# The inverse of the triangular 32x32 blocks of a gated DeltaNet chunk: five levels of small matmuls on TensorE, or forward substitution over row pairs on VectorE

## The reference

```
for layer in range(2):
    h = rms_norm(x);  proj = h @ w_in                    # 256 x 1024 times 1024 x 11024
    y_a = latent attention (4 heads)
    y_b = gated DeltaNet (4 heads of 128, chunks of 64)
    y_c = windowed attention, 3 groups of 4 heads (dilations 1, 4, 16)
    x = x + (sum of sigmoid(gate_n) * (y_n * silu(z_n)) @ w_branch[n]) @ w_out
```

```
lower = where(i > j, (k * beta) @ k.T * decay, 0)        # 64 x 64
u, w  = triangular_solve(lower + I, [v * beta, k * beta * exp(gc)])
```

## Time and profile before

| | us |
|---|---|
| median of 3 runs | 794.19 |
| span of the profiled execution | 792.5 |
| what lies around the span (difference to the median) | 1.7 |
| PE busy | 782.7 (99%) |
| DVE busy | 558.1 (70%) |
| ACT busy | 478.0 (60%) |
| POOL busy | 193.1 (24%) |
| mean granted TensorE clock | 0.997 |

### The profile page before, as it was taken

The page is one execution under the profiler, slowest core; times in us unless marked ns, Lnnn a source line. Parts: engine busy times, 40 slices in busy tenths (PEclk is TensorE's granted clock), DMA queues, the critical chain, the costliest instruction groups (busy, mean ns, idle before and its releaser), DMA issues.

```text
span 792.5 us, 15685 instructions
## 1 busy us (share of the span) xinstructions
PE 782.7 (99%) x6298; PEld 674.2 (85%) x6298; DVE 558.1 (70%) x760; ACT 478.0 (60%) x1073; POOL 193.1 (24%) x197
## 2 busy tenths in 40 slices
PE   7999999999999999999999999999999999999998
PEld 6999888878888888888899998888888888888886
DVE  6687878867476477776656886887865754958763
ACT  6869485676486654354457777764856766543551
POOL 1155104206042002321023511221331500116100
PEclk9999999999999999999999999999999999999999
DMA  8666454444463346465565563554455443664551
GB/s 236 197 192 208 157 149 133 152 153 137 133 188 122 114 144 193 123 198 173 156 195 178 160 195 108 170 172 147 130 160 139 132 137 107 183 188 140 187 181 53
DMA packets 73056, 125.16 MB, mean 158 GB/s; under 512 B 9758, under 2 KB 17048, under 8 KB 72984
## 3 DMA queue, kind: packets, MB, share of 16 engines
q1 hardware_dynamic: 72560, 124.10, 51.7%
q10 hardware_dynamic: 423, 0.06, 0.1%
HBM read 122.03 MB, written 1.05 MB: 155 GB/s over the span
## 4 chain that ended last, share of the span: by engine, by line
PE 92%; ACT 3%; DVE 2%; issue 1%; DMA 1%; SPq 0%; ACTq 0%
PE bank L781 23%; PE bank L783 22%; PE bank L782 22%; PE bank L763 3%; PE bank L765 3%; PE bank L764 3%; PE bank L868 2%; PE bank L811 2%; PE bank L921 1%; ACT w_hi L1154 1%; PE bank L882 1%; DMA xs<-in_x 1%; PE bank L916 1%; ACT at L1423 1%; PE bank L898 1%
## 5 line engine op out<-in xcount | busy, mean ns | idle before, releaser
L1488 DVE TENSOR_TENSOR w_lo<-raw,w_hi 128x1024 fp32r<-128x1024 f32 (+4 forms) x240 | 295.9, 1262 | 105.2 <-ACT w_hi L1154 102.8
L1154 ACT ACTIVATE w_hi<-raw 128x1024 fp32r<-128x1024 f32 (+4 forms) x239 | 235.1, 1018 | 89.4 <-PE bank L783 76.7
L781 PE MATMUL bank<-w_hi,hT 128*128 128x512 f32 (+2 forms) x704 | 278.5, 396 | 1.6 <-DVE mixed L1507 1.1
L783 PE MATMUL bank<-w_hi,hT 128*128 128x512 f32 (+2 forms) x704 | 271.5, 386 | 0.0
L782 PE MATMUL bank<-w_lo,hT 128*128 128x512 f32 (+2 forms) x704 | 271.1, 385 | 0.0
L781 PEld LDWEIGHTS bank<-w_hi,hT 128*128 128x128 f32 x704 | 133.5, 190 | 27.5 <-DVE mixed L1507 1.6
L783 PEld LDWEIGHTS bank<-w_hi,hT 128*128 128x128 f32 x704 | 133.1, 189 | 25.7
L782 PEld LDWEIGHTS bank<-w_lo,hT 128*128 128x128 f32 x704 | 133.5, 190 | 22.9
L1942 POOL TENSOR_TENSOR sm<-sm,tab 128x8 f32<-128x8 f32 (+3 forms) x46 | 58.5, 1271 | 184.5 <-ACT dn L1368 78.7
L763 PE MATMUL bank<-hT,w_hi 128*128 128x256 f32 x192 | 54.9, 286 | 0.0
L765 PE MATMUL bank<-hT,w_lo 128*128 128x256 f32 x192 | 54.3, 283 | 0.0
(11 more groups left out here) (233 smaller groups left out, 997.2 us busy)
## 6 DMA issues: line engine op xcount, KB each, us to landing
raw<-in_w_in SPq DMA_DIRECT2D x168, 512.0 KB, 4.5
raw<-in_w_branch SPq DMA_DIRECT2D x24, 512.0 KB, 4.3
raw<-in_w_out SPq DMA_DIRECT2D x16, 512.0 KB, 3.7
raw<-in_w_in SPq DMA_DIRECT2D x8, 384.0 KB, 5.4
raw<-in_w_in SPq DMA_DIRECT2D x8, 320.0 KB, 4.4
raw<-in_mla_w_kv_b SPq DMA_DIRECT2D x8, 256.0 KB, 3.0
raw<-in_mla_w_q_b SPq DMA_DIRECT2D x4, 384.0 KB, 3.3
xs<-in_x SPq DMA_DIRECT2D x2, 512.0 KB, 5.7
```

Source lines behind the costliest of these rows:

```text
L781: mm(o, src[0][:, a, tok], hi[:, k, :], start=starts and p == k == 0, stop=False)
L783: last = mm(o, src[1][:, a, tok], hi[:, k, :], start=False, stop=ends(u, p) and k == k1 - k0 - 1)
L1154: av(view(w_hi, q % SPLIT, k1 - k0, n), view(raw, q % RAW, k1 - k0, n), ACT.Copy).then_inc(hi_done, 1)
L1488: tt(view(w_lo, q % SPLIT, k1 - k0, n), view(raw, q % RAW, k1 - k0, n), view(w_hi, q % SPLIT, k1 - k0, n).bitcast(F32), ALU.subtract).then ...
```

## The change

The five small levels are gone from TensorE and GpSimd. VectorE inverts the 32 diagonal blocks by forward substitution. Three new steps do it.

dn_G, behind unit 25 and ahead of the scores of group 0: the blocks are turned by the vector engine's 32x32 transpose, so that each partition holds the whole matrix of one block (8 blocks of a stack, for each of four groups of 8 result columns), the factors are turned likewise and multiplied in, and two tiles of the result are set to the start values.

dn_S, eight parts behind units 26 to 33, two row pairs each, 16 pairs in all. A pair (the last has only the first of them) is three chained instructions, a multiply-add that finishes the pair's second row, a product of both rows with all rows below, and a reduce that adds them.

dn_T, behind unit 34: a copy that joins the halves, and two transposes that make T and Tt. The step is followed by dn_wide, which waited for the last dn_TX before and now waits for dn_T. dn_X and dn_TX of the level of 32 stay behind units 36 and 37. The table of constants loses the five level masks and the small identity (192 columns) and gains the start values (256).

```diff
-    put(25, ("dn_M", 0))
-
-    for s in range(len(LEVELS)):
-        put(26 + 2 * s, ("dn_X", s))
-        put(27 + 2 * s, *([("dn_M", s + 1)] if s < LAST else [("dn_kd",)] if s == LAST + 1 else []), *([("dn_T1",)] if s == 0 else []), ("dn_TX", s))
-    put(28 + 2 * LAST, ("dn_wide",))
+    put(25, ("dn_G",))
+    for n, pairs in enumerate(solve_parts()):
+        put(SOLVE_FIRST + n, ("dn_S", n))
+    put(SOLVE_FIRST + SOLVE_UNITS, ("dn_T",), ("dn_wide",))
+    put(36, ("dn_X",))
+    put(37, ("dn_kd",), ("dn_TX",))
...
+def solve_parts():
+
+    rows = list(range(0, SUB - 1, 2))
+    cuts = [round(len(rows) * n / SOLVE_UNITS) for n in range(SOLVE_UNITS + 1)]
+    return [rows[a:b] for a, b in zip(cuts, cuts[1:])]
...
             def dn_X(step, layer):
-                s = step[1]
                 b = banks(step)[0]
-                if s <= LAST:
-                    pe.wait_ge(*after("gpsimd", ("dn_M", s), layer))
...
+                pe.wait_ge(*after("vector", ("dn_T",), layer))
                 pe.wait_ge(*free(step, layer))
-                if s > LAST:
-                    last = across(b, lambda o, n, lo, hi: mm(o[hi, :], U_n[lo, n, SUB:CH], d_T[lo, n, :], start=True, stop=True))
-                else:
-                    last = by_rows(b, 0, lambda o, n, r: mm(o, d_Us[r, n, :], const("ident_c")[r, :] if s == 0 else d_T[r, n, :], start=True, stop=True))
-                last.then_inc(bank_full[b], 1)
+                across(b, lambda o, n, lo, hi: mm(o[hi, :], U_n[lo, n, SUB:CH], d_T[lo, n, :], start=True, stop=True)).then_inc(bank_full[b], 1)
...
+            def dn_G(step, layer):
+
+                dve.wait_ge(*after("scalar", ("dn_Uc",), layer))
+                if layer == 0:
+                    dve.wait_ge(start["tab_loaded"], 16)
+                blocks_of = d_Uc.rearrange("p n i -> p i n").unsqueeze(2).broadcast_to([P, SUB, GROUPS_OF, NT * H])
+                nc.vector.transpose(g_L.rearrange("p m i -> p i m"), blocks_of)
+                own_next(nc.vector.transpose(g_b, brk.rearrange("p t h -> p (t h)").unsqueeze(1).broadcast_to([P, GROUPS_OF, NT * H])), layer)
+                stt(g_L, g_L, -1.0, g_b.unsqueeze(1).broadcast_to([P, SUB, SUB]), ALU.mult, ALU.mult)
+                for v in g_T:
+                    last = nc.vector.tensor_copy(v, const("first").rearrange("p (i j) -> p i j", i=SUB))
+                own_next(last, layer)
+
+            def dn_S(step, layer):
+
+                for k in solve_parts()[step[1]]:
+                    j, v = k // GROUPS_OF + 1, k // 2 % 2
+                    old, new = g_T[v], g_T[1 - v]
+                    own_next(stt(old[:, k + 1, 0:j], old[:, k, 0:j], g_L[:, k, k + 1:k + 2], old[:, k + 1, 0:j], ALU.mult, ALU.add), layer)
+                    if k + 2 == SUB:
+                        continue
+                    shape = [P, 2, SUB - k - 2, j]
+                    own_next(tt(planes[v][:, 1:3, k + 2:, 0:j], g_L[:, k:k + 2, k + 2:].unsqueeze(3).broadcast_to(shape),
+                                old[:, k:k + 2, 0:j].unsqueeze(2).broadcast_to(shape), ALU.mult), layer)
+                    own_next(nc.vector.tensor_reduce(new[:, k + 2:, 0:j], planes[v][:, :, k + 2:, 0:j].rearrange("p c i j -> p i j c"), AX.X, ALU.add), layer)
+
+            def dn_T(step, layer):
+
+                own_next(nc.vector.tensor_copy(g_rows[0], g_rows[1]), layer)
+                own_next(nc.vector.transpose(d_T.rearrange("p n (j r) -> p j r n", r=GROUPS_OF), g_T[0].rearrange("p i j -> p j i")), layer)
+                nc.vector.transpose(d_Tt.rearrange("p n i -> p (n i)"), d_T.rearrange("p n j -> p (n j)")).then_inc(part("vector", step), 1)
```

More of the change, by code:

```diff
@@ L328 @@
                   ("inv_n", GROUPS), ("inv_d", 1), ("inv_hd", 1), ("inv_rope", 1), ("eps", 1), ("eps_hd", 1), ("half", 1), ("q_scale", 1),
[L329 to L330 removed]
+                  ("qk_scale", 1), ("power", 1), ("chunk", 2), ("one", 1), ("tri", P), ("same", P), ("not_tri", CH), ("first", SUB * EACH), ("mask_m", 2 * P), ("mask_0", 2 * P), *[(f"mask_{a}", P) for a in APART]):
     TAB[_name] = (_at, _n)
@@ L361, in shape_tables @@
     put("not_tri", np.where(pc <= jc, 0.0, NEG))
[L362 to L369, removed]
+    row, column = np.divmod(np.arange(SUB * EACH)[None, :], EACH)
+    put("first", row == column * GROUPS_OF + i % SUB // EACH)
     for a, prev in (("m", j >= 0 * i), (0, j >= i)):
@@ L1030, in dn_u @@
                 wait_taken(step, layer, ("dn_bT", 2, t))
-                pe.wait_ge(*taken(("dn_TX", LAST + 1), layer))
+                pe.wait_ge(*taken(("dn_TX",), layer))
                 pe.wait_ge(*after("scalar", ("dn_wide",), layer))
@@ L1331, in dn_wide @@
             def dn_wide(step, layer):
-                act.wait_ge(*taken(("dn_TX", LAST), layer))
+                act.wait_ge(*after("vector", ("dn_T",), layer))
                 for c in range(2):
@@ L1340, in dn_kd @@
             def dn_kd(step, layer):
-                act.wait_ge(*full(("dn_X", LAST + 1), layer))
+                act.wait_ge(*full(("dn_X",), layer))
                 act.wait_ge(*taken(("dn_qk",), layer))
@@ L1880, in _ @@
                      "dn_g1": dn_g1, "dn_gc": dn_gc, "dn_row": dn_row, "dn_cv": dn_cv, "dn_silu": dn_silu,
-                     "dn_bT": dn_bT, "dn_bE": dn_bE, "dn_decay": dn_decay, "dn_kkE": dn_kk, "dn_qkE": dn_qk, "dn_X": dn_X, "dn_T1": dn_T1, "dn_TX": dn_TX, "dn_wide": dn_wide, "dn_ws": dn_ws, "dn_ds": dn_ds, "dn_oc": dn_oc, "dn_o": dn_o, "dn_oss": dn_oss,
+                     "dn_bT": dn_bT, "dn_bE": dn_bE, "dn_decay": dn_decay, "dn_kkE": dn_kk, "dn_qkE": dn_qk, "dn_G": dn_G, "dn_S": dn_S, "dn_T": dn_T, "dn_X": dn_X, "dn_TX": dn_TX, "dn_wide": dn_wide, "dn_ws": dn_ws, "dn_ds": dn_ds, "dn_oc": dn_oc, "dn_o": dn_o, "dn_oss": dn_oss,
                      "b_out": b_out, "k_norm": k_norm, "sc": sc, "soft": soft,
@@ L2058, in dn_ss @@
                 last.then_inc(part("gpsimd", step), 1)
-            def dn_M(step, layer):
-                s = step[1]
-                if layer == s == 0:
-                    pool.wait_ge(start["tab_loaded"], 16)
-                pool.wait_ge(*(after("scalar", ("dn_Uc",), layer) if s == 0 else full(("dn_X", s - 1), layer)))
-                tt(d_Us, d_Uc, const(f"levelT{LEVELS[s]}").unsqueeze(1).broadcast_to([P, NT * H, SUB]), ALU.mult).then_inc(part("gpsimd", step), 1)
             def dn_dec(step, layer):
```

72 lines of the change are left out of this document (21 added, 51 removed).

## The result

The changed kernel takes 786.54 us (median of 4 runs) against 794.20 for the kernel before on the same chip: ratio 0.990, 95% interval 0.9887 to 0.9914, faster by 7.7 us. The forecast was 785.4. One of the four executions, the profiled one, ran at a lower granted clock throughout (849.63 us, mean clock 0.849), so the ratio goes by the other three (median 786.24), and all rows "after" come from a second run of the same kernel (786.73 us, ratio 0.9912, 0.9896 to 0.9929, span 784.6).

What follows compares the result with a forecast made beforehand. TensorE, busy 782.7 of 792.5 us, was taken as the bound. Per layer 7.6 gained less 2.9 delay and 0.3 margin gives 4.4, 8.8 in all: 794.19 to 785.4, range 781 to 790 (chance 0.55).

Steps and rivals of the forecast that it cites:

- The gain: Dropping ten groups of small matmuls (dn_X, dn_TX, levels 0 to 4) frees TensorE of 9.9 us per layer.
- the rival of the full gain: All ten groups count, since dn_G is cheaper or ScalarE's chain has play: 2 x 9.9 us, 774.4; chance 0.12.
- The place of dn_G: Ahead of group 0's scores, dn_G delays ScalarE by 3.05 us, so unit 27 starts at 176.2 instead of 173.13.
- The size of dn_G: On VectorE, dn_G's transposes, multiply-add and copies take 3.05 us, range 2.5 to 4.3; large transpose 1.22.
- pv 2.9 us late: TensorE's pv waits for ScalarE's copy of the weights and starts at 182.4, not 179.48: 2.9 us lost per layer.
- The groups from there on: After pv, dropped groups bring TensorE forward: dn_X at 0.78 each, dn_TX at 1.30, together 7.6 us per layer.
- The wait ahead of unit 33: TensorE waits about 0.7 us for ScalarE to free the bank, so dropping level 3's dn_X yields only 0.1.
- the 0.3 that I had taken off for margins: Allowance per layer for tight w_lo pieces, solve part 5 and GpSimd contention: gain 4.4 us instead of 4.7.
- The solve: On VectorE, dn_S takes 13.2 us per layer in eight chained parts of 0.8 to 2.1, nearly all hidden.
- The slower rival: VectorE becomes the stretch's bound, slower from 0.55 us per short instruction; 799 at 0.6, 806 at 0.7; chance 0.18.
- The signs: Expected TensorE wait near 173 to 176; wrong if w_lo waits at 185 to 235 or short instructions over 0.4 us.
- No change: dn_G takes about 7 us through slow transposes, so delayed scores eat the gain: 794; chance 0.15 including small gains.

Runs made afterwards that it cites:

- without the solve: Changed kernel with dn_G and dn_S left out, start values copied in dn_T so the 32x32 inverses stay identities: 774.56 us, 0.9758 of the kernel before.
- the kernel at 778.92: Changed kernel with dn_G moved behind the first scores of group 0 and the first solve part behind the second scores: 778.92 us, 0.9812 of the kernel before.
- The padded run: Changed kernel, order kept, with 46 extra chained one-element instructions per layer in dn_S (8.7 us per layer): 804.99 us, 1.0134 of the kernel before.
- the kernel at 790.80: Changed kernel with dn_G in its place, the solve's parts one unit later (units 27 to 34) and dn_T behind 35: 790.80 us, 0.9957 of the kernel before.
- the padded kernel of the other order: Changed kernel with the 46 extra instructions, dn_G and all solve parts behind their unit's other steps, parts one unit later: 800.02 us, 1.0078 of the kernel before.

## Why the prediction was right, point by point

**The gain, right in sum, by two errors that cancel.** Ten groups at 9.9 us per layer; without the solve the runs show (794.0 - 774.56) / 2 = 9.7. But the groups were worth 10.8 on TensorE, and 1.5 came back as waits for ScalarE, which the rival of the full gain, with all ten groups counting, had left out.

**The place of dn_G, right.** The step was: dn_G delays the scores, these ScalarE, this unit 27 and pv. All links are in the timelines, and moving dn_G alone gives back 6.6 us of the 12 that the work on VectorE costs. Moving the first solve part as well gives another 1.2. ScalarE's idle became 6.77 instead of 5.9.

**The size of dn_G, too small.** 3.94 against 3.05. The mis-sized term is the large transpose, 2.19 us here (2188 ns on average over the two layers) against 1.22. I had chosen the row of a contiguous operation for an instruction that reads a broadcast and writes with a stride; my upper bound of 2.3 held it. The rule that I cited, the Trainium skill, Vector Engine (DVE) Microarchitecture Reference, section "The reshape front-end and per-opcode configuration", one element per cycle and lane, agrees with the contiguous form (1246 ns, the multiply-add of as many elements 1225) and not with the strided ones (1901 to 1998).

**pv 2.9 us late, in fact 4.65.** Before the stretch the changed kernel is 0.49 us ahead (its scores on TensorE start at 162.72, those of before at 163.21; the runs do not say from what, and without the solve the same scores start at 161.98), so pv is 183.64 + 0.49 - 179.48 = 4.65 late. Of the 1.75 too much, 0.9 is dn_G and 0.3 the first solve part (1.81 against 1.5). The clock lengthens unit 27 to pv by 7.05 - 5.58 = 1.5 us, which the prediction had put at nothing; only 183.64 - 183.29 = 0.35 of it shows, since pv had to wait for ScalarE's copy anyway. Some 0.2 is spread over other rows.

**The groups from there on, 0.65 us better than thought.** From pv to the dn_X at unit 36 the kernel goes from 4.16 us late (183.64 against 179.48) to 4.09 early (245.25 against 249.34), 8.25 us instead of 7.6. The starts around a group say why: from pv to pv it is 187.17 - 179.48 = 7.69 before with a dn_X between, 6.82 after (183.64 to 190.46), so 0.87 and not 0.78. With a dn_TX between it is 196.38 - 187.17 = 9.21 before and 198.26 - 190.46 = 7.80 after, so 1.41 and not 1.30. I had read the gap alone; the matmuls around it come closer together too (0.1 of it in pv). The wait ahead of unit 33 is there with 0.86 (0.7 forecast). Together a layer gains 3.85 us (the first scores of layer 1 start 385.65 behind those of layer 0, before 389.5) instead of 4.4: 8.25 - 4.65 = 3.6 here and 0.25 elsewhere in the layer. So the forecast, 1.1 us off, is nearer than its terms, and that is luck: against 1.75 too little delay stand 0.65 too little gain, the 0.25 and the 0.3 that I had taken off for margins.

**The solve, longer and still nearly free.** dn_S is 17.3 us per layer instead of 13.2. The shortest instructions cost what I took (0.22 for one element, forecast 0.21); three multiply-adds and a product per layer are held by GpSimd to about 1.0 us each, some 3 us, in parts 1, 3 and 7, which the prediction had named. This lock is what the Trainium skill states in SBUF — State Buffer, section "SBUF: two separate sides", and the runs bear it out for products (1.07 us at 187.59, 0.27 for the same one in the kernel at 778.92), multiply-adds (1.00 against 0.22) and w_lo (3.93 against 2.36). Longer as it is, the solve costs 0.3 to 0.6 us per layer.

**The slower rival: its price was too low.** I put the point from which it is slower at 0.55 us for each short instruction. In the changed kernel the 46 take 17.3 us, 0.38 each. The padded run adds 0.19 to that, so it lies at 0.57 and not at the 0.48 of its expectation, and it is slower than before by 1.3%. That it is slower fits the threshold. How much does not: between 794 at 0.55 and 799 at 0.6 the prediction would have it near 796, and it takes 805. Between 0.38 and 0.57 there is no run, so where the two kernels would be equal is not known. The missing term is what the added work does to others: 8.7 us per layer cost TensorE 9.15 in the first order and 7.8 in the other. The busy share of 75% over the program does not show how little was left. The one of the stretch does, 68.5 of 76.9 us: 8.4 us, less than was added. From the first scores to the dn_X of unit 36 VectorE's busy time grew by 14.4 us (58.6 to 73.0), not by 10.9.

**The signs.** TensorE has no wait for w_lo between 185 and 235, and the wait at 176 is there. Apart from the held ones no instruction of dn_S takes over 0.43 us (the longest reduces do).

**No change, and dn_G at 7 us:** not so; full gain: not so in this order, but within 4.4 us of it in the best.

## What to carry to other kernels

Work moved to an idle engine costs by what stands behind it in that engine's fixed order. Look first for the instruction whose consumer is already idle (here the scores, ScalarE's 2.81 us), and put new work behind it, but not where another engine's shared access begins. A wait of the bounding engine can cost more than its length, since the clock may fall behind it (by 2.5 and 1.5 us in the two layers of the kernel at 790.80). Judge the room on an engine by its busy time in the stretch, not over the program. Price an instruction by a row with the same access pattern, not only the same number of elements.

## What the runs showed of the hardware

After a wait of 3.34 us the granted clock fell to the lower level for 6 to 13 matmuls of 512 columns, which started 0.43 us apart instead of 0.23: the unit's 24 matmuls took 6.96 to 8.27 us instead of 5.58, so 1.4 to 2.7 us more. Filling the wait removed that whole. How long it lasted differed between kernels and between the two layers of one execution with the same wait (8.11 and 7.04 us in one, 8.27 and 6.96 at unit 33 of the padded one); why is open. Of two waits of 1.27 us in one execution one was followed by it and the other by full clock. In the padded kernel of the other order it followed the waits of 3.38 and 3.36 us and not those of 1.90 to 2.58.

A 32x32 transpose of 1024 f32 elements takes 1.25 us contiguous and 1.9 to 2.0 with a stride on one side or both; one of 256 takes 0.45 contiguous and 0.68 strided. A chained instruction of one element takes 0.16 to 0.22 us, and the next starts 0.03 after its end. A short VectorE instruction with two inputs from SBUF took up to 0.9 us more where a scaling of GpSimd ran beside it, two w_lo pieces 1.6 us more, and a copy of 128 elements, which has one input, 1.06 us in the kernel at 790.80 against 0.22.
